# Moving the second layer's first modulation units from the first router into the first mixer's output projection

## The chip, the cores and the metric

The kernel runs on one core of one Trainium2 chip. Its engines are TensorE (PE, and PEld for its weight loads), VectorE (DVE), ScalarE (ACT), GpSimd (POOL) and SyncE (SP, whose queue issues most transfers). The metric is device time in microseconds. Before the change it is 3133.79 us, the median of 3 runs (3133.17 to 3140.09).

## The reference, cut to what matters

The model is two blocks in a row. The first has two layers; each has a mixer and a mixture of experts, and each is steered by modulation vectors that depend only on the condition vectors `c` and `c_ctx` and on the weights:

```python
for layer in range(2):
    sh1, sc1, g1, sh2, sc2, g2 = split(silu(c) @ mod_w[layer] + mod_b[layer], 6)
    h = rmsnorm(x) * (1 + sc1) + sh1
    x = x + g1 * mixer(h)          # layer 0: Fourier and convolution, layer 1: attention
    h2 = rmsnorm(x) * (1 + sc2) + sh2
    x = x + g2 * hier_moe(h2)      # router, top 2 of 32 experts, blocks of rows per expert
```

In layer 0 this is done for 512 tokens and 256 context tokens, 768 in all. `mod_w[layer]` is 1024 x 6144 float32. The kernel cuts it into 12 units of 512 columns (2 MB each); units 0 to 3 hold `sh1` and `sc1`. Units 0 to 3 of layer 1 depend on nothing that layer 0 computes, and are needed first when layer 1's mixer begins.

## The kernel before

Every engine runs a program written out by hand, and the engines wait for each other on semaphores. Transfers are issued in program order from SyncE's queue; a wait there holds back everything behind it. Gathers by index come from GpSimd.

**Memory.** `ring` has 6 slots of 4096 columns (2 MB over 128 partitions). An expert has three matrices of 2 MB, gate, up and down; `expert_slot(kind, b)` puts those of block 0 in slots 3, 4, 5, of block 1 in 0, 1, 2, of block 2 in 3, 4, 5 again. So a matrix of block b + 2 can be fetched only when TensorE is through with the same one of block b. `scr` is scratch memory. PSUM has 8 banks that `Banks.take` hands out in turn; a bank taken with `hold=True` is skipped until it is released.

**A modulation unit** takes, for each half of its rows, one load of 1 MB and `pe_mod_half` (line 519): 4 matmuls of 512 columns, each with a stationary operand of 32 columns, on the four strips of the array. The profile shows 8 instructions of form 128*32 for a half, since a float32 matmul is two of them. ScalarE copies the result (`mod_row`), TensorE turns it into columns (`pe_mod_turn`, 4 matmuls of 2 columns, 8 instructions), ScalarE copies these (`mod_columns`).

**The first mixer** (`sp_fourier`, `pe_fourier`, `act_fourier`, `dve_fourier`) has an input projection, Fourier and convolution steps, and an output projection. The output projection goes over m = 0 to 7 and, for each m, over chunks of 512 and 256 columns: 24 matmuls of split float32 parts each (`pe_product8`), group name `f_o`. Its weights are jobs 6 to 9 of 1 MB, in slots 3, 4, 5 and 3; job 9 can be loaded when m = 1 is over. Slot 0 holds the Fourier step's intermediate result and is not in use after group (`f_y`, 0, 3). The units 4 to 11 of layer 0 are already worked off between groups of the input projection, through the two halves of slot 2.

**The first mixture of experts** (`sp_moe`, `pe_moe` and so on with l = 0). TensorE makes the norm's sum and its roots, then `pe_router`: logits (`r_l`, 8 tiles of hT by 512 and by 256 columns, a tile as soon as ScalarE has scaled and shifted it), their turn (`r_t`), transposed rows of h (`rows(i)`, written to `hrows` in memory by GpSimd), counts and ranks (`r_n`, `r_k`, `r_p`), each after a stretch of small VectorE steps, and the assignment of rows to blocks (`r_r`: 12 matmuls of 47 columns, 24 instructions; 8 of 40 columns in layer 1). VectorE turns the result into indices; GpSimd gathers the rows of block 0, and TensorE transposes them (`x_tr`) and begins with `pe_blocks`. Blocks 0, 1, 3, 7 and six more are wide (128 rows), the others have 64 rows.

The four units of layer 1 stand in this router: unit 0 ahead of the logits, unit 1 after `r_t`, unit 2 between turns 0 and 1 after the last `rows(i)`, unit 3 and turns 2 and 3 after `r_r`. Their loads go through two buffers in `scr`. SyncE issues gate of expert 0 behind unit 0's loads, then units 1 to 3, then waits for block 0's gathered rows, and only then issues gate, up and down of expert 1. In layer 1, which has no units in its router, gate and up of expert 1 are issued right behind expert 0's gate. Experts from the third on are fetched by GpSimd with indirect transfers (`pool_blocks`).

## Time and profile before

| | |
|---|---|
| median of 3 runs | 3133.79 us (3133.17 to 3140.09) |
| span of the profiled execution | 3128.6 us |
| median of the runs less this span | 5.2 us |
| mean granted clock of TensorE | 0.953 of full speed |
| busy: PE / DVE / ACT / POOL | 2872.3 / 1077.5 / 747.1 / 504.6 us |
| output projection | 230 to 295 us |
| first router, up to block 0's first expert matmul | 296 to 350 us |
| first expert blocks | 350 to 886 us |

The time of the profiled execution is its span, from the first to the last instruction, and the 5.2 us that lie around it in a timed run. Times in the rows are in us from the span's start. Engine busy time is no proof of a bound: an engine that waits inside a stage may still set that stage's end. A row of the view in order of time has the start, the duration, engine, line, operation, output<-inputs, shape, count, and in brackets the idle time before it with what ended it. Line 92 is the helper that issues every matmul, line 95 every transpose, so groups are told apart by tiles and shapes: 128*32 is a modulation half, 128x2 a turn, 128*64 from hT the logits, 128x47 the assignment of rows.

### The profile page before, as it was taken

Reading aid. Unit: us, or ns where it says so; the run is one execution under the profiler, and the core shown is the slowest. Engines: PE = TensorE matmul, PEld = TensorE weight load, DVE = VectorE, ACT = ScalarE, POOL = GpSimd, SP = SyncE. Lnnn points to the kernel's source line nnn. Section 1 sums busy time; section 2 is a strip of 40 time slices with the busy share of each in tenths; the row PEclk is TensorE's granted clock in tenths of the full one; section 3 lists DMA queues with packets and bytes.
Section 4 is the critical chain, followed back from the end, with each engine's and each line's share of the span. In section 5 each row is a group of like instructions: output and inputs, shape, how many; then the busy total and the mean of one; then the engine's idle time right before and its main releaser. Section 6 shows DMA issues by size and latency. Waiting matters only on the chain.

```text
span 3128.6 us, 37290 instructions
## 1 busy us (share of the span) xinstructions
PE 2872.3 (92%) x15950; PEld 2013.4 (64%) x15950; DVE 1077.5 (34%) x2064; ACT 747.1 (24%) x1305; POOL 504.6 (16%) x503
## 2 busy tenths in 40 slices
PE   6989898899969899979998996999999989999997
PEld 4777655445547665765644554888875556788876
DVE  4973300000034544330000003433356654433334
ACT  4142210111123144321111112332201165321323
POOL 0000132323210033112332221000033041000000
PEclk9999999999989999979999997999999999999998
DMA  7613899999952133259999994232311201232321
GB/s 271 201 44 130 322 386 403 402 389 398 407 191 68 56 108 108 81 206 368 411 418 402 402 414 163 81 108 94 111 58 55 96 19 55 94 98 91 108 83 46
DMA packets 143404, 621.56 MB, mean 199 GB/s; under 512 B 14447, under 2 KB 95471, under 8 KB 109568
## 3 DMA queue, kind: packets, MB, share of 16 engines
q0 software_dynamic: 40160, 403.75, 32.0%
q1 hardware_dynamic: 101920, 210.35, 19.7%
q10 hardware_dynamic: 1152, 4.98, 0.4%
q8 instruction: 130, 2.13, 0.3%
q14 instruction: 42, 0.34, 0.0%
HBM read 612.73 MB, written 29.36 MB: 205 GB/s over the span
## 4 chain that ended last, share of the span: by engine, by line
PE 73%; DMA 15%; DVE 6%; ACT 2%; issue 2%; POOL 1%; SPq 0%; DVEq 0%; POOLq 0%; ACTq 0%
PE ps L92 70%; DMA ring<-in_exp_up,wix 13%; PE ps L95 2%; DVE scr L114 2%; DVE scr L106 1%; ACT hT L98 1%; DVE scr L120 1%; DMA scr<-in_mod_w 1%; DMA ring<-in_mod_w 1%; DVE ring_r L106 1%; DMA ring<-in_exp_down,wix 0%; DVE hT_r L106 0%; POOL ring L135 0%; DVE scr L117 0%; DVE hT L114 0%
## 5 line engine op out<-in xcount | busy, mean ns | idle before, releaser
L92 PE MATMUL ps<-ring_r 128*128 128x512 f32 (+1 forms) x2688 | 778.7, 376 | 22.4 <-DVE hT_r L106 21.7
L92 PE MATMUL ps<-ring,scr 128*64 128x512 f32 (+4 forms) x3072 | 700.8, 572 | 85.1 <-DMA ring<-in_exp_up,wix 64.5
L92 PEld LDWEIGHTS ps<-ring_r 128*128 128x128 f32 x2688 | 496.8, 191 | 129.9 <-issue 35.2
L92 PEld LDWEIGHTS ps<-ring,scr 128*64 128x64 f32 (+2 forms) x3072 | 256.3, 146 | 440.7 <-issue 434.2
L92 PE MATMUL ps<-hT_r,ring_r 128*128 128x512 f32 (+1 forms) x1256 | 472.8, 376 | 0.0
L92 PE MATMUL ps<-scr,ring 128*128 128x128 f32 (+1 forms) x2784 | 332.4, 282 | 20.5 <-DMA ring<-yrows 16.7
L92 PEld LDWEIGHTS ps<-scr,ring 128*128 128x128 f32 x2784 | 320.2, 194 | 30.4 <-issue 28.3
L106 DVE TENSOR_TENSOR scr<-scr,ps 64x512 f32<-64x512 f32 (+1 forms) x76 | 52.5, 690 | 782.2 <-ACT scr L98 454.2
L92 PE MATMUL ps<-scr_r,ring_r 128*128 128x512 f32 x1312 | 306.7, 390 | 0.3 <-issue 0.3
L92 PEld LDWEIGHTS ps<-scr_r,ring_r 128*128 128x128 f32 x1312 | 246.3, 188 | 52.3 <-issue 0.5
L92 PEld LDWEIGHTS ps<-hT_r,ring_r 128*128 128x128 f32 x1256 | 240.5, 191 | 43.4 <-issue 1.8
L106 DVE TENSOR_TENSOR ring_r<-ring,ring_r 128x2048 fp32r<-128x2048 f32 (+1 forms) x98 | 216.7, 2235 | 73.6 <-ACT ring_r L102 73.2
L102 ACT ACTIVATE ring_r<-ring 128x2048 fp32r<-128x2048 f32 (+1 forms) x102 | 186.3, 1834 | 180.2 <-DMA ring<-in_ffn_w 131.5
L98 ACT ACTIVATE scr<-ps 64x512 f32<-64x512 f32 (+2 forms) x96 | 56.0, 584 | 679.8 <-PE ps L92 679.8
L102 ACT ACTIVATE scr<-ps 128x512 f32<-128x512 f32 (+2 forms) x200 | 107.9, 548 | 446.9 <-PE ps L92 305.2
L92 PE MATMUL ps<-ring 128*64 128x128 f32 (+10 forms) x904 | 135.7, 401 | 17.8 <-ACT scr L102 10.4
L103 DVE COPY scr<-ps 128x512 f32<-128x512 f32 (+3 forms) x102 | 54.4, 548 | 258.2 <-PE ps L92 173.1
L106 DVE TENSOR_TENSOR scr<-hT,ps 128x512 f32<-128x512 f32 x44 | 30.3, 688 | 313.1 <-PE ps L92 313.1
L95 PEld LDWEIGHTS ps<-KC,scr 64*128 64x128 f32 (+2 forms) x878 | 77.8, 139 | 92.7 <-issue 76.9
L102 ACT ACTIVATE ring<-ps 128x512 f32<-128x512 f32 (+4 forms) x171 | 73.8, 462 | 196.8 <-PE ps L92 152.8
L92 PEld LDWEIGHTS ps<-ring 128*64 128x64 f32 (+4 forms) x904 | 78.2, 163 | 61.3 <-issue 35.0
L135 POOL DMA_INDIRECT ring<-in_exp_gate,wix x60 | 58.0, 967 | 330.5 <-PE ps L92 304.8
(147 smaller groups left out, 2570.0 us busy)
## 6 DMA issues: line engine op xcount, KB each, us to landing
ring<-in_ffn_w SPq DMA_DIRECT2D x66, 1024.0 KB, 5.5
ring<-in_mod_w SPq DMA_DIRECT2D x12, 2048.0 KB, 8.2
ring<-in_mod_w SPq DMA_DIRECT2D x16, 1024.0 KB, 5.1
ring<-in_exp_up SPq DMA_DIRECT2D x4, 2048.0 KB, 13.3
ring<-in_exp_down SPq DMA_DIRECT2D x4, 2048.0 KB, 8.6
scr<-in_mod_w SPq DMA_DIRECT2D x8, 1024.0 KB, 7.8
ring<-in_exp_gate SPq DMA_DIRECT2D x4, 2048.0 KB, 12.1
ring<-in_w_in SPq DMA_DIRECT2D x4, 2048.0 KB, 8.3
```

The costliest lines, as they stand in the source:

```text
L92: return self.real.matmul(o, l, r, start=start, stop=stop) if self.real else Quiet()
L95: return self.real.transpose(o, i, identity) if self.real else Quiet()
L98: return self.real.activation(o, i, f, **how) if self.real else Quiet()
L102: return self.real.activation(o, i, ACT.Copy) if self.real else Quiet()
L103: return self.real.tensor_copy(o, i) if self.real else Quiet()
L106: return self.real.tensor_tensor(o, a, b, op) if self.real else Quiet()
L114: return self.real.scalar_tensor_tensor(out=o, in0=a, scalar=s, in1=b, op0=op0, op1=op1) if self.real else Quiet()
L120: return self.real.reciprocal(o, i) if self.real else Quiet()
L135: return self.real.indirect_dma_start(out=o, out_offset=None, in_=table, in_offset=bass.IndirectOffsetOnAxis(ap=idx, axis=0), **bound) if ...
```

## The change

The four units of layer 1 (`mod1`, in the same scratch area as the first layer's units) leave the router and go between the groups of the first mixer's output projection. After the first chunk of each m, TensorE works off half m % 2 of unit m // 2; after the second chunk of m = 2, 4 and 6 it turns the unit before, and after m = 7 the last one. ScalarE copies the row after the first chunk of odd m, the columns after the second chunk of m = 2, 4, 6 and at the end. SyncE loads the halves into the two halves of slot 0, from the moment the Fourier step has left it; each load waits until the half that was there before is used. In the router nothing of the units is left; gate and up of expert 1 are issued behind gate of expert 0 in layer 0 too, and its down after the gather of block 0's rows, as before. GpSimd no longer waits for the last unit before it gathers block 2's rows.

```diff
@@ -311,7 +311,7 @@
 
     ps = Banks([ctx.enter_context(nc.psum_tensor(f"ps{i}", [128, 512], F32))[:, :] for i in range(8)],
                signal("bank_full"), [signal(f"bank{i}_free") for i in range(8)])
-    wr = Slots([signal(f"slot{i}_landed") for i in (0, 1, 2, 3, 4, 5, "2_half0", "2_half1", "_piece0", "_piece1", "_windows")], ps)
+    wr = Slots([signal(f"slot{i}_landed") for i in (0, 1, 2, 3, 4, 5, "2_half0", "2_half1", "0_half0", "0_half1", "_windows")], ps)
     pe_stage, dve_stage, act_stage, pool_stage = (signal(f"{x}_stage_done") for x in ("pe", "dve", "act", "pool"))
     vec_in, const_in, x_in, out_done = (signal(x) for x in ("vec_in", "const_in", "x_in", "out_done"))
     squared, summed, rooted, inverse = (signal(x) for x in ("squared", "summed", "rooted", "inverse"))
@@ -617,6 +617,7 @@
     s_ = Scratch(F.s.at)
     mod0 = Mod("first", 0, [0, 1, 2, 3], s_)
     mod0b = Mod("rest", 0, list(range(4, 12)), Scratch(F.s.at), "first")
+    mod1 = Mod("next", 1, [0, 1, 2, 3], Scratch(F.s.at), "first")
     st_x0 = Stat("x0", F.pa[:, 0:768], [F.pa[:, 768:1280], F.pa[:, 1280:1792]], X, by_tile(8, 768), 768, F.rs0)
 
 
@@ -624,6 +625,9 @@
 
     def mod_half(u, half):
         return lambda kt: slot(2, 2048 * half + 512 * (kt % 4), 512)
+
+    def next_half(half):
+        return lambda kt: slot(0, 2048 * half + 512 * (kt % 4), 512)
 
     def after_group(m, g):
 
@@ -672,8 +676,21 @@
         wr.take(1, "f_dft", 512)
         e.wait_ge(*ps.filled("f_pa", 3, 512))
         e.dma(F.dft[512].rearrange("p (k n) -> p k n", k=4), I["dft256"]).then_inc(*wr.load("f_dft", 512))
-        for j in range(8, 10):
-            job(j)
+        def next_load(u, half):
+            wr.take(8 + half, "next_half", u, half)
+            e.wait_ge(*wr.open("next_half", u, half))
+            e.dma(slot(0, 2048 * half, 2048).rearrange("p (k n) -> p k n", k=4), I["mod_w"][1, u][:, 4 * half:4 * half + 4, :]
+                  ).then_inc(*wr.load("next_half", u, half))
+        job(8)
+        e.wait_ge(*ps.filled("f_y", 0, 3))
+        for half in range(2):
+            next_load(0, half)
+        next_load(1, 0)
+        job(9)
+        next_load(1, 1)
+        for u in (2, 3):
+            for half in range(2):
+                next_load(u, half)
 
     def pe_product8(e, o, key, step, c, x, a, n, lo_of, order=range(8)):
 
@@ -782,8 +799,16 @@
                 o = ps.take("f_o", m, a)
                 e.wait_ge(*ps.ready("f_o", m, a))
                 pe_product8(e, o, ("f", j), 256, 128 * (m % 2), f_mix, a, n, "f_mix", (4, 5, 6, 7, 0, 1, 2, 3)).then_inc(*ps.fill("f_o", m, a))
+                if a == 0:
+                    u, half = m // 2, m % 2
+                    e.wait_ge(*wr.there("next_half", u, half))
+                    pe_mod_half(e, mod1, u, half, next_half(half))
+                    wr.done(("next_half", u, half), "mod", 1, u, by=None if half else pe_step)
+                elif m % 2 == 0 and m:
+                    pe_mod_turn(e, mod1, m // 2 - 1)
             if m % 2:
                 wr.done(("f", j), "f_o", m, 512)
+        pe_mod_turn(e, mod1, 3)
         stage_end(e, "f", "act", "dve")
 
     def act_fourier(e):
@@ -869,8 +894,13 @@
             for a, n in chunks(768):
                 e.wait_ge(*ps.emptied("f_o", m, a))
                 act_square(e, st_f, m, a, n)
+                if a == 0 and m % 2:
+                    mod_row(e, mod1, m // 2)
+                elif a and m % 2 == 0 and m:
+                    mod_columns(e, mod1, m // 2 - 1)
             if m == 1:
                 part_upper(e, ("f", 9))
+        mod_columns(e, mod1, 3)
         stage_end(e, "f", "dve", "pe")
 
     def dve_fourier(e):
@@ -1045,9 +1075,7 @@
             u = Scratch(at)
             self.oa, self.wr = [u(NT * 128) for _ in range(2)], u(512)
             self.ob = scr[:, 0:2 * NT * 47]
-            self.half = [scr[:, at + 2048 * i:at + 2048 * i + 2048] for i in (1, 2)]
             assert u.at <= at + 2048 and 2 * NT * 47 <= self.T
-            self.mod = Mod("next", 1, [0, 1, 2, 3], Scratch(F.s.at), "first") if l == 0 else None
             assert s.at <= (F.s.at if l == 0 else NSCR), s.at
 
     moes = [Moe(0), Moe(1)]
@@ -1126,9 +1154,6 @@
 
         return moes[l].hst[:, 1024 * i:1024 * i + 1024] if i < 2 else slot(expert_slot(2, 1), 1024 * (i - 2), 1024)
 
-    def mod_piece(u, half):
-        return lambda kt: moes[0].half[half][:, 512 * (kt % 4):512 * (kt % 4) + 512]
-
     def sp_moe(e, l):
         M = moes[l]
         def fixed(b, *kinds):
@@ -1136,13 +1161,6 @@
                 weights_load(e, expert_slot(kind, b), ("e", l, kind, b),
                              I[f"exp_{('gate', 'up', 'down')[kind]}{l}"].rearrange("(e p) n -> e p n", p=128)[b], 1, 4096)
 
-        def mod_load(u):
-            for half in range(2) if l == 0 else ():
-                wr.take(8 + half, "mod_piece", u, half)
-                e.wait_ge(*wr.open("mod_piece", u, half))
-                e.dma(M.half[half].rearrange("p (k n) -> p k n", k=4), I["mod_w"][1, u][:, 4 * half:4 * half + 4, :]
-                      ).then_inc(*wr.load("mod_piece", u, half))
-
         fixed(0, 1, 2)
         e.wait_ge(*act_stage.of(("f", "at")[l]))
         e.wait_ge(*dve_stage.of(("f", "at")[l]))
@@ -1150,17 +1168,15 @@
         e.dma(M.wr.rearrange("p (k n) -> p k n", k=8), I["router_w"][l]).then_inc(*router_in.up(l, "w", by=16))
         e.dma(M.rb, I["router_b"][l]).then_inc(*router_in.up(l, "b", by=16))
 
-        mod_load(0)
         fixed(0, 0)
-        for u in (1, 2, 3):
-            mod_load(u)
-        if l == 1:
-            fixed(1, 0, 1)
+        if l == 0:
+            e.wait_ge(*ps.filled("mod", 1, 3))
+        fixed(1, 0, 1)
         for i in (M.NT - 2, M.NT - 1):
             e.wait_ge(*rows_out[i % 2].of(l, i))
 
         e.wait_ge(*xg_in[0].of(l, 0))
-        fixed(1, *(range(3) if l == 0 else (2,)))
+        fixed(1, 2)
 
         for b in range(FIXED, M.NB):
             for kind in range(3):
@@ -1177,18 +1193,9 @@
                         e.dma(moe_y(l, i, q)[:, 512 * h:512 * h + 512], yrows[r:r + 128, 512 * h:512 * h + 512]).then_inc(
                             *y_in[a, h].up(l, i, q, by=16))
 
-    def pe_mod_pieces(e, u):
-        M = moes[0]
-        for half in range(2):
-            e.wait_ge(*wr.there("mod_piece", u, half))
-            pe_mod_half(e, M.mod, u, half, mod_piece(u, half))
-            wr.done(("mod_piece", u, half), "mod", 1, u, by=None if half else pe_step)
-
     def pe_router(e, l):
         M = moes[l]
         NT, T = M.NT, M.T
-        if l == 0:
-            pe_mod_pieces(e, 0)
         e.wait_ge(*router_in.of(l, "b"))
 
         for a, n in chunks(T):
@@ -1215,8 +1222,6 @@
                 for j in range(4):
                     m = e.transpose(o[:, 128 * j:128 * j + 128], H(4 * q + j, 128 * i, 128), k("id"))
                 m.then_inc(*ps.fill("r_h", l, i, q))
-        if l == 0:
-            pe_mod_pieces(e, 1)
         for i in range(3):
             rows(i)
 
@@ -1237,10 +1242,6 @@
         e.matmul(o[:, 0:160], k("ones")[0:32, :], M.rows[0:32, :], True, True).then_inc(*ps.fill("r_p", l))
         for i in range(4, NT):
             rows(i)
-        if l == 0:
-            pe_mod_turn(e, M.mod, 0)
-            pe_mod_pieces(e, 2)
-            pe_mod_turn(e, M.mod, 1)
 
         o = ps.take("r_r", l)
         e.wait_ge(*ps.ready("r_r", l))
@@ -1251,23 +1252,15 @@
                 m = e.matmul(o[:, 0:M.NB], M.oa[q][:, 128 * i:128 * i + 128], M.ob[:, n:n + M.NB], q + i == 0,
                              q == 1 and i == NT - 1)
         m.then_inc(*ps.fill("r_r", l))
-        if l == 0:
-            pe_mod_pieces(e, 3)
-            pe_mod_turn(e, M.mod, 2)
-            pe_mod_turn(e, M.mod, 3)
 
     def act_router(e, l):
         M = moes[l]
         NT = M.NT
-        if l == 0:
-            mod_row(e, M.mod, 0)
         e.wait_ge(*router_in.of(l, "b"))
         for a, n in chunks(M.T):
             e.wait_ge(*ps.filled("r_l", l, a))
             e.activation(M.lt[:, a:a + n], ps.ap("r_l", l, a)[:, 0:n], ACT.Identity, bias=M.rb).then_inc(
                 *ps.empty("r_l", l, a))
-        if l == 0:
-            mod_row(e, M.mod, 1)
 
         for i in range(NT):
             for q in range(2):
@@ -1276,13 +1269,6 @@
         e.wait_ge(*dve_step.of(l, "w2"))
         e.activation(M.gt, M.gt, ACT.Exp)
         e.activation(M.w2, M.w2, ACT.Exp).then_inc(*act_step.up(l, "w2"))
-        if l == 0:
-            mod_columns(e, M.mod, 0)
-            mod_row(e, M.mod, 2)
-            mod_columns(e, M.mod, 1)
-            mod_row(e, M.mod, 3)
-            mod_columns(e, M.mod, 2)
-            mod_columns(e, M.mod, 3)
 
     def pool_router(e, l):
         M = moes[l]
@@ -1641,8 +1627,6 @@
         def store(b):
             pool_outputs(e, l, b, *y_out[b % 2].up(l, b, by=16))
         for b in range(3):
-            if l == 0 and b == 2:
-                e.wait_ge(*ps.filled("mod", 1, 3))
             fetch_x(b)
         e.wait_ge(*dve_step.of(l, "rows"))
         for b in range(32):
@@ -1763,7 +1747,7 @@
                 d = e.ts(moe_diag(l, i, q), k("id"), w[:, i, :], MUL)
         d.then_inc(*dve_step.up("diag", l))
         if l == 0:
-            dve_mod_bias(e, M.mod)
+            dve_mod_bias(e, mod1)
         late = []
         for r, (a, n) in enumerate(chunks(M.T)):
             for c in range(8):
```

## Rows read from the trace of the kernel before

**Rows 1.** The page's fourth part: shares of the chain that ended last, by engine.

```profile
PE 73%; DMA 15%; DVE 6%; ACT 2%; issue 2%; POOL 1%; SPq 0%; DVEq 0%; POOLq 0%; ACTq 0%
```

**Rows 2.** Stretches: length, busy us (instructions) of PE, PEld, DVE, ACT, POOL, clock, DMA share, GB/s.

```profile
230.00:296.00 66.00, 65.53 (x379) 57.35 (x379) 23.00 (x35) 14.88 (x23) 0.00 (x0) 1.00 0.23 80
296.00:350.00 54.00, 41.51 (x272) 26.07 (x273) 30.36 (x98) 22.22 (x45) 6.84 (x10) 0.80 0.75 274
...
390.00:392.00 2.00, 2.00 (x12) 0.61 (x10) 0.64 (x1) 0.00 (x0) 1.42 (x2) 1.00 0.46 82
...
400.00:477.00 77.00, 77.00 (x478) 47.34 (x477) 6.36 (x11) 8.36 (x14) 23.27 (x24) 1.00 1.00 398
...
477.00:882.00 405.00, 367.57 (x2008) 196.35 (x2008) 33.28 (x56) 43.58 (x73) 110.14 (x114) 0.95 0.96 391
```

**Rows 3.** TensorE in order of time, input projection (start us, duration).

```profile
90.38 0.28 PE L92 MATMUL ps<-hT_r,ring_r 128*128 128x256 f32 x1
90.50 0.28 PE L92 MATMUL ps<-ring_r 128*128 128x256 f32 x1
...
91.70 0.38 PE L92 MATMUL ps<-ring_r 128*128 128x256 f32 x1
...
100.37 1.84 PE L92 MATMUL ps<-AM,scr 128*128 128x2 f32 x16
102.14 1.06 PE L92 MATMUL ps<-ring,scr 128*32 128x512 f32 x8
```

**Rows 4.** The chain of waits in the first router (start us, us, what).

```profile
299.77 8.62 DMA scr<-in_mod_w
...
335.38 8.76 DMA scr<-in_mod_w
```

**Rows 5.** TensorE in order of time, first router.

```profile
310.29 6.14 PE L92 MATMUL ps<-hT,scr 128*64 128x512 f32 x32
...
337.45 3.76 PE L92 MATMUL ps<-scr 128*128 128x47 f32 x24 [1.16 <-DVE scr L106]
...
347.85 1.07 PE L95 MATMUL ps<-KC,scr 128*128 128x128 f32 x8
349.75 16.00 PE L92 MATMUL ps<-scr,ring 128*128 128x128 f32 x128 [0.83 <-ACT scr L102]
```

**Rows 6.** ScalarE in order of time, first router.

```profile
301.97 8.60 ACT L98 ACTIVATE hT<-hT,MT 128x512 f32<-128x512 f32 x16 [3.24 <-DVE hT L114]
```

**Rows 7.** TensorE's groups from 310 to 317 (busy us, mean ns of one).

```profile
L92 PE MATMUL ps<-hT,scr 128*64 128x256 f32 x16 | 1.9, 379 | 0.0
```

**Rows 8.** Stretches of the second router, columns as in rows 2.

```profile
1342.00:1346.00 4.00, 4.00 (x11) 1.98 (x10) 2.96 (x5) 3.72 (x6) 0.00 (x0) 0.50 0.99 418
1346.00:1350.00 4.00, 2.78 (x18) 1.64 (x15) 0.11 (x1) 0.69 (x1) 0.00 (x0) 0.99 1.01 434
...
1366.00:1370.00 4.00, 3.34 (x16) 3.37 (x16) 1.27 (x3) 0.00 (x0) 0.00 (x0) 0.50 0.00 0
```

**Rows 9.** TensorE and GpSimd in order of time, second router.

```profile
1341.26 6.32 PE L92 MATMUL ps<-hT,scr 128*64 128x512 f32 x16 [1.75 <-ACT hT L98]
...
1366.66 3.60 PE L92 MATMUL ps<-scr 128*128 128x40 f32 x16 [5.97 <-DVE scr L106]
...
1372.13 1.09 POOL L135 DMA_INDIRECT scr<-hrows,scr  x1 [10.89 <-DVE scr L120]
...
1378.73 16.87 PE L92 MATMUL ps<-scr,ring 128*128 128x128 f32 x128 [0.98 <-DVE scr L103]
```

**Rows 10.** GpSimd and SyncE in order of time, and landings of unit loads, first router.

```profile
343.14 1.10 POOL L135 DMA_INDIRECT scr<-hrows,scr  x1 [9.45 <-DVE scr L120]
...
347.49 0.33 SPq L132 DMA_DIRECT2D ring<-in_exp_gate  x1
...
358.87 0.96 POOL L135 DMA_INDIRECT ring<-in_exp_gate,wix  x1 [8.12 <-PE ps L92]
...
DMA to landing us min/median/max: 5.2/7.8/9.1
```

## Prediction

> **What bounds the kernel now.** I read the chain that ended last first, because it says which engine holds each stretch: TensorE holds most of the span and transfers 15% [rows 1]. Then I cut the part that the change touches into stretches [rows 2]. Three things are to be seen. From 230 to 296, the output projection, TensorE is busy for 65.53 of 66.00 us at a granted clock of 1.00 (its higher level, 2.4 GHz), while the DMA share is only 0.23: what is added there on TensorE costs its full duration, what is added on the DMA engines costs nothing yet. From 296 to 350, the router, TensorE is busy for 41.51 of 54.00 us at a mean clock of 0.80, and the DMA engines carry the four units. From 350 on the expert blocks run: TensorE is full until 477 (77.00 of 77.00 us from 400), and from 477 to 882 it has holes (367.57 of 405) while the DMA share stays at 0.96. The last thing to read in these rows is the point where the DMA engines ran dry: in 390 to 392 they moved 82 GB/s at a share of 0.46, against 398 GB/s at 1.00 later. That point decides this case.
>
> **Part 1: the units' matmuls enter the projection.** The input projection of the same layer already has such pieces between its groups, so it has their price [rows 3]. Without a piece, instructions of 256 columns start 0.12 us apart (90.38, 90.50). With a piece of one half the next one starts at 91.70, 1.20 after 90.50: one half costs 1.08 us. Eight halves cost 8.6. Two turns in a row start at 100.37 and the half behind them at 102.14, so two turns take 1.77 and four take 3.5. Sum: 12.1, and 12.2 with the break of a stream at single turns. The last turn (after m = 7) lies ahead of the norm's sum, which TensorE runs without a break, so it counts too. Bounds: 11.5 if the turns overlap with products, 13 if each break costs 0.1 more. TensorE's idle time in this stretch is 0.47 us in all, so nothing covers it.
>
> **Part 2: the units leave the router's front.** The chain shows 8.62 us on the landing of the first unit [rows 4]. That is what it waited for, not what it gains. When the piece is over and the logits start at 310.29 [rows 5], ScalarE is still at the last tile of hT, which ends at 301.97 + 8.60 = 310.57 [rows 6]. Without the piece the logits of the first chunk run tile by tile as hT comes (every 1.07 us), and only the last tile's 512 columns and the second chunk stay behind 310.57. Now the logits end at 310.29 + 6.14 = 316.43. Their price by clock: in the second layer's router, which has no such piece, 8 products of 512 columns took 6.32 us, nearly all at a clock of 0.50 (1.2 GHz) [rows 8, 9], so 0.79 each where two share the array, and 1.6 for one alone; in this router the second chunk took 1.9 [rows 7], at the higher level. At the higher level the end is 310.57 + 0.8 + 1.9 = 313.3, 3.1 earlier; at the lower it is 310.57 + 1.6 + 3.2 = 315.4, 1.0 earlier. In the second layer the clock stood at 0.50 in the first half of the logits and at 0.99 behind them [rows 8]; here they begin near 303, with more of them behind that change, so I take 2.5, nearer the higher level.
>
> **Part 3: the middle and the tail of the router.** Units 1 and 2 fill waits for VectorE and leave no gap in its own chain, so their removal gains nothing there. But TensorE then idles ahead of the row assignment, as in the second layer. There 16 instructions took 3.60 us, 0.225 each, at a clock of 0.50; here 24 took 3.76, 0.157 each [rows 5, 8, 9]. All 24 at 0.225 are 5.4: 1.6 later (bounds 0 and 1.6; I take 1.6, since the idle time ahead grows from 1.16 us to about 4.9 once unit 2 (1.9) and two turns (1.8) are gone, and it was 5.97 there). The Trainium skill ("TensorE: Matmul & The Clock Gate", "What's actually happening") states that the throttled clock is the default and that activity releases it, which speaks against taking filler matmuls out of a stage that waits; the trace agrees, by the 0.225 against 0.157. By the rule this term is the 1.6 taken; if the clock did not depend on the filler it would be 0, and the sum 10.6.
>
> The last unit's landing at 344.13 stands in the chain with 8.76 us [rows 4], but beside it runs a second thing: the gather of block 0's rows, issued at 343.14, landed by 347.49, when SyncE, which waits for it, issued the next load [rows 10]. TensorE began the transposes at 347.85 [rows 5]. From the gather to the first expert matmul it is 6.61 us here (343.14 to 349.75) and 6.60 in the second layer (1372.13 to 1378.73), where there are no units [rows 5, 9, 10]: gain 0, at best 0.5, the time from the landing to the transposes. Block 0's gate and up, 16.00 here, took 16.87 there with the lower clock at their start: 0.9 later, bounds 0 and 0.9. Tail: 1.6 + 0 + 0.9 = 2.5 later.
>
> **Part 4: the transfers.** What moves: eight loads of 1 MB go from 299 to 344 into 220 to 285, and gate and up of the second expert (2 MB each) are issued behind the first's gate, not at 347.49 [rows 10]. The gain can only be in a stretch where the DMA engines set the pace. They don't until 477: TensorE runs without a hole from 400 to 477 [rows 2], because each gather needs a slot that TensorE frees. The gather for block 2 goes out at 358.87, when block 0's gate product is over [rows 10]. The old order's backlog, those two loads, was gone at 390 [rows 2]. From there both kernels have the same transfers outstanding at the same distance from block 0's start, so the gain is 0. The other end of the bound is in the first rival.
>
> **What costs nothing, and its cover.** On SyncE's queue the last loads of the units stand ahead of the first expert's up and down, and so put up off from the end of m = 3 to that of m = 5, about 285 here; it is needed at block 0's start, 350 and later, and even the slowest unit load took 9.1 us to land for 1 MB [rows 10], so its 2 MB are there by 305. The projection's last weight load stands behind one unit load whose wait ends with m = 0, so it is issued where it was; sharing the engines with one more load may cost 2.6 us of landing, hidden by some 25 us until m = 6. Each unit load has two steps of m, some 16 us by the 66 us of eight steps, for a landing of 5 to 9 us (7.8 at the median [rows 10]); if that cover were gone, TensorE would stop for the difference. The PSUM bank that is held leaves seven for groups that VectorE empties within one step. ScalarE gets four copies of 0.60 and four of 0.18 us, and is busy for 14.88 of 66.00 us. GpSimd loses a wait on the last unit ahead of the third gather, needed 30 us later. The bias addition on VectorE stays.
>
> **Sum.** 12.2 - 2.5 + 2.5 = 12.2 us later. The profiled span is 3128.6 us; the median of the runs is 3133.79, so 5.2 lie around the span and stay. Forecast 3133.8 + 12.2 = 3146.0. With all bounds at their low ends 11.5 - 3.1 - 0.5 = +7.9, at their high ends 13 - 1.0 + 1.6 + 0.9 = +14.5: its own range is 3141 to 3149.
>
> **Rivals.** (a) The backlog counts. If the DMA engines have no slack between 350 and 882, the 4.2 MB that gate and up take out, at 398 GB/s, give back 10.5 us: 12.2 - 10.5 = +1.7, 3135.5. For it: a share of 1.00 from 400, and the 15% of the chain that are transfers. Against it: the 82 GB/s at 390. It decides if the DMA engines do not empty before the first stall. (b) The chain at its word: both waits for units, 8.62 + 8.76 = 17.4, were real and block 0 starts that much earlier; with the last unit's matmuls and turns (a half at the lower clock, 1.9, and two turns, 1.8) gone too, 12.2 - 17.4 - 3.7 = -8.9, 3124.9, faster. It decides as soon as the waits save more than 12.2. For it: the chain. Against it: hT's end at 310.57 and the gather's landing, which leave at most 3.1 and 0.5 us to gain. (c) The unit loads come late in the projection, because the queue's waits are in order: if the eight landings each miss by about 1 us, 8 more, 3154. For it: the expert's up is in the same queue; against it: 16 us for each, and the first pair is issued four Fourier groups and a whole product group ahead of its use.
>
> **Chances.** Forecast 0.72, (a) 0.12, (b) 0.06, (c) 0.10. A measurement of this kernel tells no change from one of 0.2%, 6.3 us, so the bounds are 3127.5 and 3140.1. (b) is faster; (a) reaches into either side, 0.02 of it faster; with its rest and a thin tail of the forecast 0.12 is within. Faster 0.08, same 0.12, slower 0.80. The range 3135 to 3150 holds the forecast's own range, most of (a) and the lower part of (c).
>
> **What would show it.** The projection should end some 12 us later with TensorE busy throughout and 64 instructions of 128*32 in it; the logits should follow the last hT activation by 2.5 to 4 us; the row assignment should take about 5.4 us at a clock of 0.50; the gap from block 0's gather to its first expert matmul should be 6 to 7 us; the DMA rate should fall well below 300 GB/s in the first 40 us of the blocks; and the stretch from block 0's start to the layer's end should be unchanged within 1 us. It is wrong if that last stretch shrinks by several us (a), if block 0 starts earlier than at 349.75 (b), or if TensorE waits for unit loads in the projection (c).

## Result and the profile after

The changed kernel takes 3143.43 us (median of 14 runs, 3138.32 to 3152.47) against 3133.88 us for the kernel before (14 runs): a ratio of 1.0036 with a 95% interval of 1.0027 to 1.0044, so 8.5 to 13.8 us slower, 11.3 at its middle. The profiled execution has a span of 3141.6 us, 13.0 more than that of the kernel before. The forecast was 3146.0 in a range of 3135 to 3150. Medians here and below are over the fast executions; two slow ones, of 4209.65 and 14474.99 us, one each of the kernels "second expert late" and "first halves three times", are left out.

The chain that ended last looks as before [rows 1], which says little:

```profile
PE 72%; DMA 16%; DVE 6%; ACT 2%; issue 2%; POOL 1%; SPq 0%; DVEq 0%; POOLq 0%; ACTq 0%
```

The stretches of the changed kernel, columns as in [rows 2], answer more:

```profile
230.00:308.00 78.00, 77.88 (x468) 60.82 (x468) 22.68 (x35) 16.73 (x29) 0.00 (x0) 1.00 0.41 149
308.00:362.20 54.20, 34.77 (x181) 25.55 (x181) 30.33 (x98) 19.75 (x38) 6.73 (x10) 0.78 0.53 199
362.20:402.00 39.80, 38.81 (x287) 34.94 (x288) 2.07 (x3) 3.08 (x6) 5.57 (x6) 0.95 0.74 267
402.50:404.50 2.00, 2.00 (x11) 0.73 (x12) 0.69 (x1) 0.00 (x0) 1.05 (x2) 1.00 0.08 33
...
412.50:490.00 77.50, 77.50 (x480) 47.61 (x479) 6.44 (x12) 8.36 (x14) 23.19 (x24) 1.00 1.00 400
490.00:895.00 405.00, 366.10 (x2014) 196.73 (x2013) 33.19 (x56) 43.50 (x73) 110.48 (x115) 0.96 0.97 391
```

The projection now takes 78 us instead of 65, with TensorE busy throughout, a clock of 1.00 and the DMA share up from 0.23 to 0.41. In the router TensorE is busy for 34.77 us instead of 41.51, at a clock of 0.78. The first 40 us of the blocks show the backlog gone, 267 GB/s at a share of 0.74, where the kernel before had:

```profile
350.00:385.00 35.00, 34.01 (x278) 32.42 (x279) 2.07 (x3) 2.81 (x5) 5.49 (x6) 0.96 0.99 383
```

The DMA engines run dry at 403, 41 us into the blocks, as they did 41 us into them before. Then come 400 GB/s at a share of 1.00, as before.

TensorE in order of time, from the last step of the projection to block 0's first transposes, the first expert matmuls in the fence behind it:

```profile
302.70 0.39 PE L92 MATMUL ps<-ring_r 128*128 128x512 f32 x1
303.02 1.06 PE L92 MATMUL ps<-ring,scr 128*32 128x512 f32 x8
304.01 0.39 PE L92 MATMUL ps<-ring_r 128*128 128x256 f32 x1
304.23 0.28 PE L92 MATMUL ps<-hT_r,ring_r 128*128 128x256 f32 x1
...
306.87 0.28 PE L92 MATMUL ps<-ring_r 128*128 128x256 f32 x1
306.99 0.95 PE L92 MATMUL ps<-AM,scr 128*128 128x2 f32 x8
308.05 0.38 PE L92 MATMUL ps<-KC 128*128 128x6 f32 x2
...
316.00 10.18 PE L92 MATMUL ps<-hT,scr 128*64 128x512 f32 x32 [1.30 <-ACT hT L98]
...
347.46 5.32 PE L92 MATMUL ps<-scr 128*128 128x47 f32 x24 [5.62 <-DVE scr L106]
359.24 1.97 PE L95 MATMUL ps<-KC,scr 128*128 128x128 f32 x8 [6.46 <-DMA scr<-hrows,scr]
```

```profile
362.20 16.41 PE L92 MATMUL ps<-scr,ring 128*128 128x128 f32 x128 [0.99 <-DVE scr L103]
```

One half stands between the products at 302.70 and 304.01. A turn alone stands between the last product at 306.87 and the norm's sum at 308.05. The logits (128*64 from hT) begin at 316.00, as soon as hT does, and last 10.18 us, because they wait for it tile by tile; compare 6.14 us from 310.29 before [rows 5]. The row assignment takes 5.32 instead of 3.76, and TensorE then waits 6.46 us for the gather. ScalarE, GpSimd and SyncE in the same stretch, and the one wait for a transfer that the chain of waits has there:

```profile
314.73 8.60 ACT L98 ACTIVATE hT<-hT,MT 128x512 f32<-128x512 f32 x16 [3.24 <-DVE hT L114]
```

```profile
354.70 1.10 POOL L135 DMA_INDIRECT scr<-hrows,scr  x1 [11.00 <-DVE scr L120]
```

```profile
312.06 0.91 SPq L132 DMA_DIRECT2D ring<-in_exp_gate  x2
313.01 0.43 SPq L132 DMA_DIRECT2D ring<-in_exp_up  x1
```

```profile
354.70 4.49 DMA scr<-hrows,scr
```

Measured from the projection's first full product (230.37 before, 230.06 after), the way to the first expert matmul is 119.38 us before and 132.14 after. In a second and a third profile of the changed kernel it was 132.14 and 131.91. So the projection is 13.1 us longer (77.99 against 64.92), and the router, from the norm's sum to the first expert matmul, is 0.3 us shorter without its units (54.15 against 54.46). The blocks, from there to the first matmul of the combination, took 552.74 before and 552.09 after.

### The profile page after: what moved, and what is told of

It reads as the page before. It is cut to its first block, busy times and chain, and to the rows that moved or that the text cites. A ratio compares the mean times of both kernels' runs of the same rounds, so it can differ in the third digit from the quotient of the medians.

```text
span 3141.6 us, 37290 instructions
## 1 busy us (share of the span) xinstructions
PE 2880.1 (92%) x15950; PEld 2020.1 (64%) x15950; DVE 1076.5 (34%) x2064; ACT 746.2 (24%) x1305; POOL 503.4 (16%) x503
## 4 chain that ended last, share of the span: by engine, by line
PE 72%; DMA 16%; DVE 6%; ACT 2%; issue 2%; POOL 1%; SPq 0%; DVEq 0%; POOLq 0%; ACTq 0%
PE ps L92 70%; DMA ring<-in_exp_up,wix 15%; PE ps L95 2%; DVE scr L114 2%; DVE scr L106 1%; ACT hT L98 1%; DVE scr L120 1%; DMA ring<-in_mod_w 1%; DVE ring_r L106 1%; POOL ring L135 0%; DVE hT_r L106 0%; DVE hT L114 0%; DVE scr L117 0%; DVE xT L114 0%; POOL ring L110 0%
## 5 line engine op out<-in xcount | busy, mean ns | idle before, releaser
L95 PE MATMUL ps<-KC,scr 64*128 64x64 f32 (+2 forms) x878 | 104.2, 254 | 12.4 <-DMA scr<-hrows,scr 11.8
## 6 DMA issues: line engine op xcount, KB each, us to landing
ring<-in_exp_up SPq DMA_DIRECT2D x4, 2048.0 KB, 13.8
```

Of the source, the lines that this page charges most:

```text
L95: return self.real.transpose(o, i, identity) if self.real else Quiet()
```

## Experiments

Each kernel was timed against the kernel before on the same chip. The rows of "first halves three times" are those of a second execution of it. "To block 0" is the way from the projection's first full product to the first expert matmul; "blocks" is from there to the first matmul of the combination, in one profiled execution.

| kernel | median us | ratio to the kernel before (95%) | to block 0 | blocks |
|---|---|---|---|---|
| before | 3133.88 | 1 | 119.38 | 552.74 |
| changed | 3143.43 | 1.0036 (1.0027 to 1.0044) | 132.14 | 552.09 |
| changed, again | 3144.41 | 1.0026 (1.0012 to 1.0041) | 132.14 | 553.48 |
| second expert late | 3143.83 | 1.0037 (1.0021 to 1.0054) | 132.19 | 557.91 |
| before, second expert early | 3138.91 | 1.0017 (1.0003 to 1.0031) | 126.80 | 550.05 |
| first halves three times | 3151.45 | 1.0051 (1.0036 to 1.0065) | 139.05 | 556.69 |
| changed + filler | 3141.07 | 1.0032 (1.0018 to 1.0045) | 130.70 | 553.87 |
| unit 0 early and moved | 3133.37 | 0.9997 (0.9985 to 1.0009) | 122.37 | 555.60 |
| unit 0's loads early | 3131.25 | 0.9989 (0.9978 to 1.0001) | 118.69 | 557.66 |
| units through two pairs of buffers | 3129.83 | 0.9988 (0.9977 to 0.9999) | 116.91 | 555.40 |
| the same, second expert early | 3135.56 | 1.0009 (1.0000 to 1.0018) | 121.90 | 555.57 |
| changed, a third time | 3144.82 | 1.0042 (1.0025 to 1.0059) | 131.91 | 555.60 |
| changed + filler, again | 3139.74 | 1.0027 (1.0014 to 1.0039) | 130.64 | 547.29 |

**The changed kernel again.**

> The changed kernel itself, as the control of this group of runs: each other kernel is read against it and against the kernel before on the same chip. My account: +8 to +13 us against the kernel before (part 1 measured +13.1 in the trace, the router's front -3.0, the row assignment +1.6, the way to block 0 +0.9, the blocks about 0). If the longer profiled time came from the one execution that was profiled, it would be near +9.

Measured: 1.0026, at the low end, with the same 132.14 us to block 0 in the profile.

**The second expert's loads late again**, all else as changed:

```diff
         if l == 0:
             e.wait_ge(*ps.filled("mod", 1, 3))
-        fixed(1, 0, 1)
+        else:
+            fixed(1, 0, 1)
...
-        fixed(1, 2)
+        fixed(1, *(range(3) if l == 0 else (2,)))
```

> The changed kernel with the second half of the change undone: gate and up of the second expert go out after the gather of block 0's rows, as before the change. My account (the old backlog is gone 40 us into the blocks): no difference from the changed kernel, within 3 us, and the DMA share between 2 and 40 us into the blocks rises from 0.74 to about 0.98. The rival (the backlog counts, 4.2 MB at 398 GB/s): 10.5 us slower than the changed kernel.

The stretch from 2 to 40 us into the blocks, here and in the changed kernel profiled beside it:

```profile
362.00:400.00 38.00, 37.01 (x280) 33.19 (x280) 2.07 (x3) 2.99 (x5) 4.74 (x5) 0.97 0.94 372
```

```profile
362.00:400.00 38.00, 37.01 (x281) 33.12 (x280) 2.07 (x3) 2.99 (x5) 4.72 (x5) 0.97 0.73 263
```

The backlog is back (372 GB/s against 263) and costs nothing on the way to block 0. The median is 0.6 us below the changed kernel's, the ratio 0.0011, or 3.4 us, above, with an interval of some 7 us on either side. A loss of the full 10.5 us is hard to hold with this; one of a few us is not excluded.

**The second expert's loads early, alone in the kernel before:**

```diff
-        if l == 1:
-            fixed(1, 0, 1)
+        fixed(1, 0, 1)
...
-        fixed(1, *(range(3) if l == 0 else (2,)))
+        fixed(1, 2)
```

> The kernel before with the second half of the change alone: gate and up of the second expert are issued right behind the last unit load, some 11 us earlier than before. My account: no difference from the kernel before, within 3 us. The rival (the backlog counts): 8 to 10 us faster. A third possibility, that these loads delay the gather of block 0's rows by sharing the DMA engines with it: 1 to 4 us slower, to be seen between the gather and the first expert matmul (6.6 us before).

It is slower by 1 to 10 us, and the third possibility is the reason, larger than I had it. From the chain of waits:

```profile
341.45 11.67 DMA scr<-hrows,scr
```

The gather of block 0's rows is issued at 341.45, behind 4.2 MB of loads issued at 334, and lands 11.7 us later instead of 4.3. The way to block 0 grows by 7.4 us. How the two shared the DMA engines stands in the last section. So of the change's two halves this one is safe only where the first has cleared the DMA engines: in the changed kernel these loads go out at 312 to 313, 42 us ahead of the gather.

**Part 1 multiplied:**

```diff
+        for j in range(4 * (times - 1) if half == 0 else 0):
+            j, kt = j % 4, 4 * half + j % 4
+            e.matmul(o[32 * j:32 * j + 32, :], M.scv[:, 32 * kt:32 * kt + 32], w(kt), True, True)
         for j in range(4):
```

with `times` 3 for the units in the projection.

> The changed kernel with the suspected cost of part 1 multiplied: the four matmuls of each unit's first half are issued three times in the output projection instead of once (the two extra rounds are overwritten, so nothing else changes). That is 8 more batches of four. My account (TensorE has no cover there): 8 x 1.0 = 8 to 8.6 us slower than the changed kernel, all of it before the norm's sum. If the projection had slack (ScalarE or VectorE setting its pace): less than 4.

> The kernel with each unit's first half issued three times, once more for its trace, since the profile of its first run was not usable. From the projection's first full product to the norm's sum it is 78.0 us in the changed kernel; my account: 86 to 86.6 here.

The rows are from a second execution, of 3150.12 us. The projection is 84.80 us instead of 77.99: 6.8 us for 8 batches, all in front of the norm's sum, and the times follow (1.0051 against 1.0026 beside it, 7.0 us in the medians). That is less than the 8 to 8.6 that I expected, but not for want of load: the rows show what a batch costs in a row and what the first one costs.

```profile
232.91 0.39 PE L92 MATMUL ps<-ring_r 128*128 128x512 f32 x1
233.23 2.78 PE L92 MATMUL ps<-ring,scr 128*32 128x512 f32 x24
235.94 0.39 PE L92 MATMUL ps<-ring_r 128*128 128x256 f32 x1
...
244.16 0.39 PE L92 MATMUL ps<-ring_r 128*128 128x512 f32 x1
...
245.48 0.39 PE L92 MATMUL ps<-ring_r 128*128 128x256 f32 x1
```

Three batches in a row put 3.03 us between 232.91 and 235.94, one puts 1.32 between 244.16 and 245.48. Products of 512 columns start 0.23 apart. A batch behind another costs (3.03 - 1.32) / 2 = 0.85, a batch between products 1.32 - 0.23 = 1.09, and 0.11 more that the rows behind it show (under Part 1 below). The projection has no slack.

**The clock.** Fillers into the bank that is overwritten next:

```diff
         e.wait_ge(*ps.ready("r_r", l))
+        for _ in range(4 if l == 0 else 0):
+            e.matmul(o, k("id"), k("diag"), True, True)
...
+                if (l, b, q) == (0, 0, 0):
+                    for _ in range(6):
+                        e.matmul(o, k("id"), k("diag"), True, True)
+                    e.wait_ge(*x_in_[b % 3].of(l, b))
```

> The changed kernel with filler matmuls in the first router, whose results are overwritten: 4 of 128x512 float32 ahead of the row assignment (TensorE idles 5.6 us there) and 6 ahead of the transposes of block 0's rows (6.5 us idle). It tells whether the clock is what the units' matmuls gave the router. If it is: the row assignment falls from 5.3 to 3.8 us or less, block 0's transposes from 1.97 to about 1.1, its gate and up from 16.4 to about 14.5, so the time from the projection's first full product to the first expert matmul falls from 132.1 by 2.4 to 3.3 us, and the whole by 4 to 5 us. If the clock does not depend on them, or the fillers get in the way: no change, or up to 2 us slower.

> The changed kernel again, beside the filler kernel on the same chip. My account as before: 8 to 13 us slower than the kernel before; 132.1 us from the projection's first full product to the first expert matmul, and 16.4 for block 0's gate and up.

> The filler kernel again, beside the changed one. In the first pair of traces the end of block 0's gate and up came 3.3 us earlier against the projection's start. If this reaches the end of the kernel: 2 to 4 us faster than the changed kernel. If the blocks' DMA-bound part takes it up: no difference within 2 us.

TensorE in the second filler run:

```profile
344.76 4.01 PE L92 MATMUL ps<-scr 128*128 128x47 f32 x24 [1.25 <-DVE scr L106]
348.55 7.65 PE L92 MATMUL ps<-KC 128*128 128x512 f32 x12
356.04 1.04 PE L95 MATMUL ps<-KC,scr 128*128 128x128 f32 x8
358.06 14.53 PE L92 MATMUL ps<-scr,ring 128*128 128x128 f32 x128 [0.99 <-DVE scr L103]
```

The row assignment takes 4.01 instead of 5.33, the transposes 1.04 instead of 1.97, block 0's gate and up 14.53 instead of 16.49 beside it. The granted clock is 1.00 from 356 to 362 here; in the changed kernel it is 0.50 from 359 to 366. The way to block 0 is only 1.3 to 1.4 us shorter, because the last filler ends at 356.04, 0.9 us after the rows have landed, but with the faster block 0 its gate and up end 3.3 us earlier (3.2 in the second pair). In time the pair differs by 5.1 us in the medians and by 0.0015, 4.7 us, in the ratios, with an interval of about 6.5 on either side. The first filler run stands at 1.0032, and the changed kernel's three ratios, 1.0036, 1.0026 and 1.0042, lie on either side of it. The rows show the clock's share; that it reaches the end is likely, and not shown. The expectation of 2.4 to 3.3 us on the way to block 0 was missed.

**The front of the router.** Starting from the kernel before, with nothing added to the projection on TensorE. First unit 0's loads alone go to slot 0 during the projection:

```diff
+        e.wait_ge(*ps.filled("f_y", 0, 3))
+        for half in range(2):
+            wr.take(11 + half, "mod_piece", 0, half)
+            e.dma(slot(0, 2048 * half, 2048)...
...
-        mod_load(0)
+        mod_load(1)
         fixed(0, 0)
-        for u in (1, 2, 3):
+        for u in (2, 3):
```

> The kernel before with the loads of unit 0 moved into the projection and its matmuls left in front of the logits. It parts the wait for the landing from the work. My account: the matmuls (3.9 us at the lower clock) then end at about 306 by the clock of the kernel before, while hT is still being made until 310.6, so the logits end as in the changed kernel: 2.5 to 3 us faster than before. If the work and not the wait was the cost: less than 1 us.

VectorE takes up the logits' turn 20.33 us after the norm's sum begins, as in the changed kernel (20.32), against 23.35 before. So the 3.0 us of the front come from the wait for the landing, and the matmuls of unit 0 may stay where they are. But only 0.7 of the 3.0 arrive at block 0, in the one execution that was profiled:

```profile
335.89 1.93 PE L92 MATMUL ps<-scr 128*32 128x512 f32 x8 [0.31 <-DMA scr<-in_mod_w]
338.38 1.94 PE L92 MATMUL ps<-scr 128*32 128x512 f32 x8 [0.55 <-DMA scr<-in_mod_w]
340.24 3.58 PE L92 MATMUL ps<-AM,scr 128*128 128x2 f32 x16
343.68 1.95 PE L95 MATMUL ps<-KC,scr 128*128 128x128 f32 x8
```

The landing of the last unit did not take them: the second half starts 110.61 us after the projection's first full product, 3.2 earlier than before (113.81), and the gather is issued 3.0 earlier. The loss is behind it. From 340.24 the last turns take 3.44 us, to the transposes at 343.68, where they took 1.81 before (from 346.04 to the transposes at 347.85 [rows 5]; its row stands below), and from the transposes' start to the first expert matmul it is 2.78 us instead of 1.90. These two, 1.6 and 0.9, leave 0.7 of the 3.2. The rows had landed at 341.94, 1.7 us before TensorE came to them; before it was 0.4. What made TensorE slower is its clock. The stretches of this kernel, and under them those of the kernel before at the same work:

```profile
340.00:342.00 2.00, 2.00 (x13) 1.76 (x9) 0.25 (x2) 0.60 (x1) 0.89 (x1) 0.50 0.43 129
342.00:344.00 2.00, 2.00 (x11) 2.00 (x12) 0.00 (x0) 0.32 (x2) 0.06 (x1) 0.50 0.80 178
344.00:346.00 2.00, 1.63 (x8) 1.22 (x6) 0.34 (x1) 1.21 (x3) 0.00 (x0) 0.50 0.95 332
```

```profile
344.00:346.00 2.00, 1.82 (x8) 0.20 (x8) 1.77 (x5) 0.00 (x0) 1.27 (x2) 0.50 0.26 51
346.00:348.00 2.00, 2.00 (x22) 1.96 (x19) 0.00 (x0) 0.78 (x2) 0.95 (x1) 1.00 0.47 144
```

```profile
346.04 1.95 PE L92 MATMUL ps<-AM,scr 128*128 128x2 f32 x16
```

The clock stays at 0.50 here through turns, transposes and into block 0, and had risen to 1.00 by the turns in the kernel before. Why it rose there and not here these rows do not show: the work ahead of the turns is the same, and TensorE waits for the two halves about as long (0.31 and 0.55 us here, 0.51 and 0.51 before). So it stays open whether these 2.5 us would be lost in every execution. The time is 0.9989 of the kernel before, and the interval includes 1.

Then unit 0's and unit 1's matmuls were moved as well, behind `r_t` and behind the first three `rows(i)`:

```diff
-        if l == 0:
-            pe_mod_pieces(e, 0)
         e.wait_ge(*router_in.of(l, "b"))
...
         if l == 0:
-            pe_mod_pieces(e, 1)
+            pe_mod_pieces(e, 0)
         for i in range(3):
             rows(i)
+        if l == 0:
+            pe_mod_pieces(e, 1)
```

> The kernel before with only its loads of unit 0 moved into the idle DMA time of the projection (into slot 0), and the matmuls of units 0 and 1 moved behind the logits, where TensorE waits for VectorE; nothing is added to the projection on TensorE. My account of the front (3.0 us are gained by taking the units from in front of the logits): the logits' turn comes 3 us earlier, block 0 starts 3 to 4 us earlier than in the kernel before (119.4 us from the projection's first full product), and the kernel is 3 to 4 us faster than before and some 14 faster than the changed one. If the chain of waits was right that the landing of 8.6 us was lost: 5 to 8 us faster than before.

No gain where 3 to 4 us were expected: 0.9997, and the way to block 0 is 3.0 us longer than in the kernel before. Unit 1 is used later, so unit 2's loads are issued later, and unit 2 stands in front of the row assignment in TensorE's order:

```profile
333.92 1.94 PE L92 MATMUL ps<-scr 128*32 128x512 f32 x8 [2.64 <-DMA scr<-in_mod_w]
...
337.52 8.04 PE L92 MATMUL ps<-scr 128*128 128x47 f32 x36
```

The halves of unit 2 wait until 333.92, and the assignment (337.52, with unit 3's first half in the same row) starts 107.69 us after the projection's first full product instead of 107.08, although the front came 3 us earlier; VectorE gets its result 2.2 us later than in the kernel before: 0.6 from the later start, and 1.6 because the assignment takes 5.37 us to VectorE's next step and not 3.80. The clock is at 0.50 from 332 to 344 here.

**All loads one unit earlier:** units 0 and 2 through slot 0, 1 and 3 through the scratch buffers, TensorE's order as in the kernel before:

```diff
+    def unit_load(e, u):
+        for half in range(2):
+            wr.take((8 if u % 2 else 11) + half, "mod_piece", u, half)
+            e.wait_ge(*wr.open("mod_piece", u, half))
+            e.dma((moes[0].half[half] if u % 2 else slot(0, 2048 * half, 2048)).rearrange("p (k n) -> p k n", k=4),
+                  I["mod_w"][1, u][:, 4 * half:4 * half + 4, :]).then_inc(*wr.load("mod_piece", u, half))
```

> The units stay in the router at the places of the kernel before, but their loads alternate between the two halves of slot 0 (units 0 and 2) and the two scratch buffers (1 and 3), unit 0's in the projection. So each load can be issued one unit earlier; TensorE's order is unchanged. With unit 0's loads alone early, the front gained 3.0 us and the last unit's landing took 2.3 of them back. My account: with all loads early the 3.0 us stay, from the projection's first full product to the first expert matmul 115.5 to 117 us (119.4 before, 118.7 with unit 0 alone, 132.1 in the changed kernel), and the whole is 2.5 to 4 us faster than the kernel before. The other reading (the landing is not what held it, the lower clock ahead of block 0 is): 118 or more.

```profile
332.03 7.84 PE L92 MATMUL ps<-scr 128*128 128x47 f32 x40 [1.16 <-DVE scr L106]
...
342.68 1.29 PE L95 MATMUL ps<-KC,scr 128*128 128x128 f32 x8 [0.84 <-DMA scr<-hrows,scr]
344.81 17.13 PE L92 MATMUL ps<-scr,ring 128*128 128x128 f32 x128 [0.83 <-ACT scr L102]
```

The reason that this expectation gives, the last unit's landing, is not the one that the trace of the kernel above shows; its other case, the lower clock ahead of block 0, is. That 116.91 falls into the range given for the wrong reason is luck. Still the edit helps: TensorE goes from the row assignment into unit 3 without a wait, and is over with it before the rows land, so their landing is the limit again (0.84 us of waiting ahead of the transposes), and these take 1.29 us instead of 1.95. The way to block 0 is 116.91 us, 2.5 less than before. How much of the 1.8 us against the kernel above is owed to the clock and how much to unit 3's earlier end, these two runs do not part. The time is 0.9988 (0.9977 to 0.9999), 2.9 us less in the medians: the only kernel here whose interval leaves out 1 on the fast side, and by so little that among twelve comparisons it may be chance.

> The same, with up of the second expert issued behind the last unit load and its gate when unit 2 is through, both ahead of the gather of block 0's rows by some 7 us or more. My account: no worse than e9, and 0 to 3 us faster in the blocks: the profiles so far have 550 to 557 us from the first expert matmul to the first matmul of the combination with the early issue, and 553 to 558 with the late one. If the transfers still run when the gather is issued: up to 3 us slower on the way to block 0, as with the second expert's loads alone (38.8 us from the logits' turn to block 0 there, 31.1 before).

With the second expert's loads early in it, the kernel is slower than before at the edge of its interval. The chain of waits:

```profile
327.69 14.00 DMA hrows<-ring
```

The last write of the transposed rows, issued at 327.69, takes 14.0 us to land (4.7 at the median in the kernel before), the gather must wait for it and goes out at 342.62, and the way to block 0 is 5.0 us longer than in the kernel without these loads, more than the 3 us allowed for. The blocks take 555.57 us against 555.40: nothing is given back.

## Why the prediction was right

The direction, the size and the reason held: TensorE's work went from a stage in which it waited into one in which it was the bound. Term by term, in the profiled executions:

- **Part 1**, 12.2 expected, 13.1 measured (77.99 against 64.92 from the first full product to the norm's sum), just above the upper bound of 13. The mis-sized term is the half. I read its price up to the first product behind it, 1.08. The product after that one starts late too: 304.23 is 0.22 behind 304.01, where products of 256 columns start 0.12 apart. (It was so in the input projection, where the product behind the one at 91.70 started at 91.92.) A half costs 1.19, and eight cost some 9.5, not 8.6. The turns were right at 3.5. A turn between two groups puts 0.92 between the products on either side, which is 0.80 more than 0.12, and the next group runs 0.10 longer:

```profile
256.49 0.28 PE L92 MATMUL ps<-ring_r 128*128 128x256 f32 x1
256.61 0.95 PE L92 MATMUL ps<-AM,scr 128*128 128x2 f32 x8
257.41 0.48 PE L92 MATMUL ps<-ring_r 128*128 128x512 f32 x1
```

The last turn puts 1.18 between 306.87 and the norm's sum at 308.05. In the kernel before that gap was 0.39 without any turn, so this one costs 0.79:

```profile
294.90 0.28 PE L92 MATMUL ps<-ring_r 128*128 128x256 f32 x1
295.29 0.38 PE L92 MATMUL ps<-KC 128*128 128x6 f32 x2
```

- **Part 2**, 2.5 expected, 3.0 measured (23.35 to 20.32 us from the norm's sum to VectorE's copy of the logits' turn). The clock was at 1.00 from 316, when the logits began, so it is near the upper of the two bounds (3.1). The prediction called the second layer's logits "nearly all" at 0.50; its row has 0.99 from 1346 on, for 1.6 of their 6.3 us.
- **Part 3.** The row assignment: 1.6 expected, 1.6 measured (3.80 to 5.36 us to VectorE's next step). The ranks in the middle lost 0.3, which I had at nothing. From the gather to the first expert matmul I had 0, by the agreement of 6.61 with 6.60 in the second router; it was 7.50, 0.9 more. The second router's rows landed in less time (3.65 us from the gather to its transposes), and so hid the slower transposes; here the gather took 4.49, about as before, and the slower transposes came on top. Block 0's gate and up: 0.9 expected, 0.4 measured.
- **Part 4**, 0 expected. The profile has the blocks 0.65 us shorter, the DMA engines dry 41 us into them as before, and all gathers up to that for block 9 at the same distance from block 0's start within 0.4 us. Behind that the blocks vary: the gathers of this execution are up to 4.7 us ahead of those before, measured from block 0's start, and at the combination 0.65 are left.

Up to block 0 the unrounded terms give 13.07 - 3.03 + 1.56 + 0.31 + 0.89 = 12.8, as measured (132.14 - 119.38). The 0.4 of block 0's gate and up is part of the blocks, which are 0.65 shorter in all. The stages behind the blocks are 1.2 us longer in the profile, and the start of the projection is 0.3 earlier; TensorE has the same work there in both kernels. That makes the profile's 13.0. The forecast's 12.2 comes nearer to it than its terms do: they have errors of 0.9 (the halves), 0.9 (the gather) and 0.3 (the ranks) one way, and 0.5 (the front) and 0.5 (block 0) the other, so part of the agreement is luck. The timed ratio, 8.5 to 13.8 us, does not tell 12.2 from 13.

**Rival (a)**, the backlog, would have given back 10.5 us. Neither the late loads in the changed kernel nor the early ones in the best one show that. A smaller effect stays open: over all profiles the blocks took 547.3 to 556.7 us with the early issue (8, mean 553.1) and 552.7 to 557.9 with the late one (5, mean 555.9), while single executions of one kernel differ by up to 6.6 (547.29 and 553.87 with the filler). **Rival (b)** took the chain's waits at their word. In the changed kernel both waits are gone, and block 0 starts 12.8 us later. Taking the first wait alone away gained 3.0 us of 8.6 at the front, because the logits need hT, and 0.7 at block 0, where TensorE ran the last turns and the transposes at the lower clock. **Rival (c)** did not come: TensorE is busy for 77.88 of the projection's 78.00 us.

The rule of the Trainium skill ("TensorE: Matmul & The Clock Gate", "What's actually happening"), as the prediction told it, held in the one place where it was tried: filler matmuls brought the row assignment from 5.33 to 4.01 us and the transposes from 1.97 to 1.04.

## What to carry to other kernels

Filler work is only worth moving out of a stage if the place where it goes has idle time on the same engine: here the same matmuls cost the projection 13.1 us, and the router became only 0.3 us shorter without them, since its waits had hidden them and its clock fell behind them. If a filler's transfer is late, move the transfer and leave the work; a second pair of buffers took TensorE's waits for the units away. And when a wait is removed, read the gain where the next stage starts and not where the wait was: 8.6 us in the chain were 3.0 at the front of the router and 0.7 at block 0, since the logits have to wait for hT in any case, and the last turns and the transposes then ran at the lower clock.

## What the runs showed of the hardware

A transfer of small packets beside one of large packets gets little of the DMA engines. With 4.2 MB issued 7 us ahead of it the gather landed after 11.7 us instead of 4.3. These are the two queues of that kernel from 346 to 350: packets, MB and share of the engines of SyncE's loads (q1) and of GpSimd's gathers (q0):

```profile
q1 hardware_dynamic: 100, 1.56, 90.8%
q0 software_dynamic: 113, 0.16, 10.7%
```

They move about as many packets each, but a packet of the loads has 16 KB and one of the gathers 1.4 KB. The Trainium skill ("DMA: Bandwidth & Descriptors", "Queues, rings and completion order") says that each DMA engine goes round between the queues it has work for, a packet at a time; the trace agrees by its 100 and 113, and equal turns with such unequal packets leave the gather a tenth of the bytes. It also started late. From its issue at 341.45 to 345.5 GpSimd's queue moved no packet, 4 us, where in the kernel before the first came 1.5 to 2 us after the issue. Why it started late was not found.

In the best kernel with the early loads, all six writes of transposed rows took 11.1 to 14.0 us to land, against 3.5 to 8.5 without these loads. The last had a load of 2 MB issued 12.3 us ahead of it and another 2.2 us behind it.

Four matmuls of 32 stationary columns on the four strips cost 0.85 us behind four others and 1.19 between products of another kind.

The way to block 0 repeats within 0.3 us over executions (132.14, 132.14, 131.91). The blocks, with a DMA share of 0.97, do not: 552.09, 553.48 and 555.60 in the same three, 553.87 and 547.29 in the two filler profiles. The spans of the two filler profiles are 3140.8 and 3131.9. A single profile's span is therefore no measure of a change of 10 us in this kernel; the stretch in front of the blocks is.
